# Layer 0's gate pieces moved from the transposes into the scores, a reordered token sum in block 2, and 42 products that nobody reads ahead of waits of TensorE

## The reference, cut to what matters

```python
mod = c_act @ w_ada[l] + b_ada[l]
shift, scale, gate = jnp.split(mod, 3, axis=-1)
h = rmsnorm(x, g_pre[l]) * (1.0 + scale[:, None, :]) + shift[:, None, :]
p = h @ w_in[l]
...
s_raw = jnp.einsum("bthd,bsd->bths", qi_b, k_idx_f)
score = jnp.einsum("bth,bths->bts", w_b, jax.nn.relu(s_raw))
_, sel = lax.top_k(score, k_top)
...
x = x + gate[:, None, :] * rmsnorm(y, g_post[l])
```

## Time and profile before

| | |
|---|---|
| time of 3 runs | 3044.73 us median (3043.07 to 3046.05) |
| the profiled execution's own time | 3046.43 us |
| its span | 3044.6 us |
| granted TensorE clock, mean | 0.98 |
| TensorE busy | 2860.1 us, 94% of the span |
| VectorE busy | 1953.3 us, 64% |
| ScalarE busy | 1323.3 us, 43% |
| GpSimd busy | 1280.0 us, 42% |

### The profile page before, as it was taken

The page is one execution under the profiler, slowest core; times in us unless marked ns, Lnnn a source line. Parts: engine busy times, 40 slices in busy tenths (PEclk is TensorE's granted clock), DMA queues, the critical chain, the costliest instruction groups (busy, mean ns, idle before and its releaser), DMA issues.

```text
span 3044.6 us, 49166 instructions
## 1 busy us (share of the span) xinstructions
PE 2860.1 (94%) x19746; PEld 1749.1 (57%) x19746; DVE 1953.3 (64%) x3140; ACT 1323.3 (43%) x2341; POOL 1280.0 (42%) x1060
## 2 busy tenths in 40 slices
PE   7889998999979988999999999999999999999998
PEld 3438776874429667864466565664764444444443
DVE  3785997763589996644875665666663654444445
ACT  3353654652366646643344554454543322122222
POOL 1302482010602580012545846767661635555551
PEclk9999999999989999999999999999999999999999
DMA  8223241002201340021101111201122201111111
GB/s 292 110 70 122 84 154 52 12 22 104 94 14 43 125 139 29 12 87 59 67 29 42 70 42 42 70 31 66 43 85 110 70 28 56 56 56 44 54 44 74
DMA packets 50898, 213.45 MB, mean 70 GB/s; under 512 B 4680, under 2 KB 9968, under 8 KB 34032
## 3 DMA queue, kind: packets, MB, share of 16 engines
q1 hardware_dynamic: 42288, 195.63, 18.5%
q10 hardware_dynamic: 8384, 14.68, 1.4%
HBM read 190.36 MB, written 19.94 MB: 69 GB/s over the span
## 4 chain that ended last, share of the span: by engine, by line
PE 41%; DVE 3%; POOL 3%; ACT 2%; issue 1%; DMA 0%; ACTq 0%; POOLq 0%; DVEq 0%
PE big L284 7%; PE big L286 7%; PE big L285 7%; PE banks L284 4%; PE banks L286 4%; PE banks L285 4%; PE banks L1183 3%; POOL w_lo L596 2%; PE banks L1162 0%; PE banks L1153 0%; PE banks L1134 0%; PE banks L1164 0%; PE banks L1170 0%; DVE arena L2567 0%; DVE arena L2568 0%
## 5 line engine op out<-in xcount | busy, mean ns | idle before, releaser
L653 POOL TENSOR_TENSOR w_lo<-stage,w_hi 128x512 bf16<-128x512 f32 x340 | 429.7, 1295 | 367.3 <-ACT w_hi L1390 367.0
L646 POOL CAST w_hi<-stage 128x512 bf16<-128x512 f32 x252 | 179.6, 753 | 781.4 <-PE big L286 588.5
L284 PE MATMUL big<-w_hi,ht_hi 128*128 128x256 bf16 (+2 forms) x1280 | 358.0, 288 | 22.7 <-DVE arena L1913 4.7
L596 POOL TENSOR_TENSOR w_lo<-stage,w_hi 128x512 bf16<-128x512 f32 x174 | 249.6, 1445 | 263.6 <-ACT w_hi L1590 263.6
L285 PE MATMUL big<-w_lo,ht_hi 128*128 128x256 bf16 (+2 forms) x1280 | 357.9, 288 | 0.0
L286 PE MATMUL big<-w_hi,ht_lo 128*128 128x256 bf16 (+2 forms) x1280 | 357.8, 287 | 0.0
L284 PE MATMUL big<-ht_hi,w_hi 128*128 128x512 bf16 x816 | 310.2, 380 | 24.7 <-POOL w_lo L596 8.7
L286 PE MATMUL big<-ht_hi,w_lo 128*128 128x512 bf16 x816 | 310.0, 380 | 0.0
L285 PE MATMUL big<-ht_lo,w_hi 128*128 128x512 bf16 x816 | 309.8, 380 | 0.0
L284 PE MATMUL big<-arena,w_hi 128*128 128x512 bf16 (+1 forms) x716 | 222.5, 328 | 21.4 <-DVE arena L2154 8.4
L285 PE MATMUL big<-arena,w_hi 128*128 128x512 bf16 (+1 forms) x716 | 222.6, 328 | 0.0
(11 more groups left out here) (395 smaller groups left out, 7144.2 us busy)
## 6 DMA issues: line engine op xcount, KB each, us to landing
stage<-in_w SPq DMA_DIRECT2D x130, 1024.0 KB, 4.8
arena<-in_w_ada SPq DMA_DIRECT2D x48, 512.0 KB, 4.4
arena<-in_x SPq DMA_DIRECT2D x16, 512.0 KB, 9.2
xs<-arena SPq DMA_DIRECT2D x16, 512.0 KB, 2.6
arena<-xs SPq DMA_DIRECT2D x16, 512.0 KB, 7.2
gt<-arena ACTq DMA_DIRECT2D x16, 256.0 KB, 2.5
arena<-gt ACTq DMA_DIRECT2D x16, 256.0 KB, 2.6
out_x<-arena SPq DMA_DIRECT2D x8, 512.0 KB, 2.6
```

The source lines that it names most:

```text
L284: pe.matmul(out, ah, bh, start=start, stop=False, skip_group_check=onto)
L596: return pool.tensor_tensor(lo, x, hi, ALU.subtract)
L646: pool.tensor_copy(w_flat[0][:, w0 + c0:w0 + c1], stage[:, n % RAW_RING, c0:c1]).then_inc(s_w_hi_split, mark(s_w_hi_split, n, q))
L653: ins = pool.tensor_tensor(w_flat[1][:, w0 + c0:w0 + c1], stage[:, n % RAW_RING, c0:c1], w_flat[0][:, w0 + c0:w0 + c1], ALU.subtract)
```

## The change

Three edits come together.

1. `transpose_x` issues no pieces any more. The 16 gate pieces all run in the scores stage: 3, 3, 4, 3, 3 after blocks 2 to 6. They use `ADA2` and `cb[1]`, a ring of four semaphores of their own, and their first four transfers are issued when the transposes are done. `gate_sum(0)` and `gate_sum(1)` run on VectorE inside block 7 of the scores.
2. In block 2, round 0, VectorE makes the low halves of `t1` between `conv_2(0, 0)` and `conv_2(0, 1)`, and `xs_low(0)` moves behind the first sum of `seven("v", 0)`.
3. `bridge(g, n)` issues n float32 matmuls of 128x512 into a tile that TensorE has just taken; nobody reads them, since the next product starts the tile afresh. There are 5 ahead of `qi`, 6 and 2 ahead of the pairs of `pw2`, 4 ahead of the first logits, and 4 ahead of the last `turn_y`: 21 in each layer.

```diff
         def ada_buf(i):
-            return (ADA if i < 24 else ADA2)[:, i % 4, :, :]
+            return (ADA if i < 16 else ADA2)[:, i % 4, :, :]
+
+        def ada_in(i):
+            return s_ada_in[i % 4 + (4 if i >= 16 else 0)]
...
-            for i in range(16, 24):
-                ada(i)
             sp.wait_ge(s_rb_out, when(s_rb_out))
             sp.dma_start(TOEP, bass.AP(AP_["rb"].tensor, 0, [[1, P], [384, NH], [1, 2 * P]])).then_inc(s_toep_in, mark(s_toep_in, by=16))
             sp.wait_ge(s_gemm, when(s_gemm, "hx", 0, 1, 3))
-            for i in range(24, 28):
+            for i in range(16, 20):
                 ada(i)
...
+            def bridge(g, n):
+
+                for i in range(n):
+                    pe.matmul(g[:, 0:512], ident, con[:, 0:512], start=True, stop=True)
+
...
                     if m == 16:
+                        pe.wait_ge(s_dve_setup, when(s_dve_setup, "cb", 1))
                         ada_at["tile"] = take(pe, "c2", "gate", 0)
...
                         ins.then_inc(s_gemm, mark(s_gemm, "hx", l, half, kp))
-                        ada_pieces(l, 1)
...
-                pe.wait_ge(s_latent_dve, when(s_latent_dve, "cq_lo", l, 1))
                 for n in range(4):
                     g = take(pe, "big", "qi", l, n)
+                    if n == 0:
+                        bridge(g, 5)
+                        pe.wait_ge(s_latent_dve, when(s_latent_dve, "cq_lo", l, 1))
...
                     if tb < NT - 1:
-                        ada_pieces(l, 2 if tb < 5 else 1)
+                        ada_pieces(l, 4 if tb == 4 else 3)
...
                 for n0 in (0, 2):
                     pair = [take(pe, "big", "pw2", l, n) for n in (n0, n0 + 1)]
+                    bridge(pair[0], 6 if n0 == 0 else 2)
...
                 def logits(tb, h):
                     N = (tb + 1) * P
+                    g = take(pe, "big", "lg", l, tb, h)
+                    if tb == 0 and h == 0:
+                        bridge(g, 4)
                     pe.wait_ge(s_qt_lo, when(s_qt_lo, l, tb))
-                    g = take(pe, "big", "lg", l, tb, h)
...
                 def turn_y(tb):
 
+                    g = take(pe, "big", "yt", l, tb)
+                    if tb == NT - 1:
+                        bridge(g, 4)
                     pe.wait_ge(s_ya, when(s_ya, l, tb))
-                    g = take(pe, "big", "yt", l, tb)
...
                 if l == 0:
-                    gate_sum(0)
                     dve.wait_ge(s_ht_lo, when(s_ht_lo, "all", 0))
...
                     w = s_(S_W + tb * 8 + h)
+                    if l == 0 and tb == NT - 1 and h in (2, 4):
+                        gate_sum(h // 2 - 1)
                     dve.wait_ge(s_relu, when(s_relu, l, i))
...
-                if l == 0:
-                    gate_sum(1)
                 count(lambda j: 0.0)
...
                     conv_2(0, 0)
-                    conv_2(0, 1)
                     dve.wait_ge(s_gemm, when(s_gemm, "q", 0, 1))
                     for g in range(2):
                         sum_low(g, "t1", TSB[g])
+                    conv_2(0, 1)
...
-                xs_low(0)
+                if b:
+                    xs_low(0)
...
-                seven("v", b, hgrn, c11=(lambda: xs_low(1),))
+                seven("v", b, hgrn, c11=(lambda: xs_low(1),) if b else (lambda: xs_low(0), lambda: xs_low(1)))
```

More of the change, by code:

```diff
@@ L108, in build @@
         s_act_setup = ctx.enter_context(nc.semaphore("act_setup"))
-        s_ada_in = [ctx.enter_context(nc.semaphore(f"ada_in{i}")) for i in range(4)]
+        s_ada_in = [ctx.enter_context(nc.semaphore(f"ada_in{i}")) for i in range(8)]
         s_ada_used = ctx.enter_context(nc.semaphore("ada_used"))
@@ L491, in ada @@
                 l, n, kp = ADA_PIECES[i]
-                if i >= 4:
+                if i >= 4 and not 16 <= i < 20:
                     sp.wait_ge(s_ada_used, when(s_ada_used, i - 4))
                 sp.dma_start(ada_buf(i), AP_["w_ada"][l, kp * 2 * P:(kp + 1) * 2 * P, n * 512:(n + 1) * 512].rearrange("(k p) n -> p k n", k=2)) \
-                    .then_inc(s_ada_in[i % 4], mark(s_ada_in[i % 4], i, by=16))
+                    .then_inc(ada_in(i), mark(ada_in(i), i, by=16))
             def weights(n):
@@ L539, in _ @@
                 if n == CHUNK_AT[(0, "cv1")]:
-                    for i in range(28, 48):
+                    for i in range(20, 48):
                         ada(i)
@@ L678, in ada_piece @@
                 l, n, kp = ADA_PIECES[i]
-                pe.wait_ge(s_ada_in[i % 4], when(s_ada_in[i % 4], i))
+                pe.wait_ge(ada_in(i), when(ada_in(i), i))
                 for k in (2 * kp, 2 * kp + 1):
-                    ins = pe.matmul(g, cb[l][:, k, :], ada_buf(i)[:, k % 2, :], start=k == 0, stop=k == KT - 1)
+                    ins = pe.matmul(g, cb[i >= 16][:, k, :], ada_buf(i)[:, k % 2, :], start=k == 0, stop=k == KT - 1)
                 ins.then_inc(s_ada_used, mark(s_ada_used, i))
@@ L693, in ada_pieces @@
                     if m == 16:
+                        pe.wait_ge(s_dve_setup, when(s_dve_setup, "cb", 1))
                         ada_at["tile"] = take(pe, "c2", "gate", 0)
                     if m == 24:
-                        pe.wait_ge(s_dve_setup, when(s_dve_setup, "cb", 1))
                         ada_at["tile"] = take(pe, "c2", "gate", 1)
```

## The result

The changed kernel takes 3052.39 us (median of 9 runs, 3048.99 to 3055.20), against 3046.05 us (9 runs) of the kernel before on the same chip. The ratio is 1.0022, with an interval of 1.0014 to 1.0030: it is slower by some 6.7 us. The forecast was 3043.4 us, range 3035 to 3051, and "same" the likeliest; the result lies outside the range, on the slower side.

A forecast was written before the change was run, and what follows sets the result against it. TensorE, busy 94% of the span, was taken as the bound; minus 10.3 (opening) plus 13.8 (scores) minus 3.9 (scores' end) plus 3.1 (bridges) minus 4.0 (block 2) made minus 1.3, so 3043.4 us, range 3035 to 3051.

The forecast's parts named there:

- same: Whole kernel: a time within 0.2%, about 6 us, of the kernel before; chance 0.60.
- The opening: Layer 0's transposes without pieces: VectorE's conversion sets the pace, ending at 63.7 instead of 76.02 us; minus 10.3 net.
- The term for the clock: First projection after the opening: starts at 1.2 GHz because TensorE idles half the time; 2.0 us lost.
- The scores: Scores stage: eight more pieces at 1.72 us each, none hidden since VectorE already idles at each burst; plus 13.8 us.
- the second rival's first leg: Scores: each burst's third piece is half covered, minus 4; part of a rival near 3035 us, chance 0.24.
- The end of the scores: Ahead of conv_in: the gate_sum(1) wait goes, both sums cost 2.5 in block 7, clock gains; minus 3.9 us.
- The clock's part: Behind the last score: the 1.2 GHz stretch from 211.00 to 217.83 runs at 2.4 GHz; minus 2.2 us.
- The third rival: Layer 0 after the scores: the stall passes to VectorE's later search, 3.9 lost and 1 added; 3048 us, chance 0.10.
- The bridges: qi, pw2, first logits and last turn_y: unread products raise the clock but add their length; plus 3.1 us, both layers.
- the first rival's mechanism: At the bridges: they don't buy the clock, low stretches come from small products and stay; 3052 us, chance 0.14.
- Block 2: Block 2, first round: t1 ahead of the second convolution removes TensorE's 4.45 wait; minus 4.0 us, between minus 1 and 7.
- slowed instead: Block 2: VectorE's second convolution, taking the subtractions' place while GpSimd was idle, would be slowed; no size given.

The follow-up runs named there:

- e4_split_later: On the changed kernel, GpSimd's split of the second weight chunk put behind the end of layer 0's opening; 3047.91 us, ratio to before 1.0008.
- e1_pieces: Gate pieces, ring and both gate sums moved as in the changed kernel, no bridges, block 2 as before; 3050.75 us, ratio to before 1.0017.
- e5_open_clock: On e4_split_later, one unread 512-column product ahead of the transposes of the opening's second to eighth tile; ratio to before 1.0012.
- e9_late_halves: On e8_halves, the eight matmuls of the four early pieces placed later in the opening, plus the block 2 edit; 3035.54 us, ratio to before 0.9970.
- e6_gate_sum: On the kernel before, only the second gate sum moved from behind the last score into the last block of scores; 3042.06 us, ratio 0.9989.
- e2_bridges: On the kernel before, all the bridges alone; 3052.18 us, ratio 1.0018.
- e3_sum: On the kernel before, the block 2 edit alone (t1 ahead of the second convolution, xs_low(0) later); 3043.63 us, ratio 0.9989.
- e7_three_bridges: On the kernel before, the bridges of qi, first logits and last turn_y, none at pw2; 3046.93 us, ratio 1.0003.
- e8_halves: e1_pieces with the later second split of e4_split_later, but four pieces kept in the opening, one matmul per tile; 3045.24 us, ratio to before 0.9996.

## Why the prediction was wrong

**The opening: the failed step.** It said "1.97 per tile, 2.05 with waits between the engines", and built 63.7 us from it. The durations came from rows in which GpSimd had nothing to do. The change moves VectorE's work into the 10 us in which GpSimd splits weights, and there both get slower: five pairs of subtractions took 12.77 us (2.81, 2.48, 1.94, 3.06 and 2.48) where five times 1.28 make 6.40. So the overlap cost 6.4 us, and the tiles took 2.6 to 3.7 us each up to 62.79. `e4_split_later` takes one of the two splits away and 3.65 us with it. The sentence that the weights "are split behind other work and are no limit that I can see" looked only at when they are ready and not at what the splitting does to its neighbour.

The forecast missed by less than 6.4 only because its sum had an error the other way. It puts seven pairs of subtractions between the first and the eighth conversion. Each pair stands behind the next tile's conversion, as the two conversions at 46.01 show, so there are six: 1.2 us too much. And a tile that GpSimd leaves alone takes 1.92 us, not 2.05: 0.9 too much. VectorE was through at 67.9 us; less the 6.4 of overlap, an undisturbed opening would end near 61.5, as an estimate. That `e4_split_later` has its record at 63.68, the forecast's own number, is luck: 2.7 us of overlap are left in it, and it began 1.0 us earlier. The term for the clock (2.0) was right in size: 2.4 in the changed kernel and 2.1 in `e4_split_later`.

The Trainium skill has a rule that bears on it and that the forecast did not weigh (SBUF — State Buffer, Who interferes with whom): a VectorE instruction with two inputs in SBUF contends with a GpSimd instruction that reads SBUF, the later one is blocked until the other is done, and one with at most one SBUF input, outside the modes that use both ports, does not contend. The trace agrees: 1.65 and 1.6 us for the subtractions side by side, and an unchanged 0.80 for the conversion.

By the Trainium skill (TensorE: Matmul & The Clock Gate, Part 4), which doesn't count transposes as TensorE being busy, the low level would have lasted through all eight steps. The trace half agrees: it is low from 52.71 to 73.19, over the last three steps, but from 47.00 to 52.70 it is high. In `e1_pieces` it is low from 49.51, back at 2.4 GHz from 52.92 to 56.34 and low again behind that, with nothing but transposes on TensorE since 44.5; there the trace doesn't agree. In `e5_open_clock`, where products stand between the transposes, the projection starts low as well, behind a wait of 4.10 us; in `e9_late_halves`, where products fill most of that wait, it starts high.

**The scores: right.** Plus 13.8 for eight pieces: VectorE's idle time grew by 13.9 us. The cover was used up, and the second rival's first leg is wrong.

**The end of the scores: right in sum, wrong in one part.** The wait gave 3.0 in `e6_gate_sum`, as worked out (4.2 less 1.2). The clock's part (minus 2.2) came from elsewhere: in the changed kernel a low stretch of 3.42 us full of products is still there, behind waits of 1.41 and 1.50 us. The shift fell by 2.1 nevertheless, because a second stretch, 309.99 to 313.40 of before, isn't in the changed kernel. The forecast did not know of that one. The third rival, that the stall passes to VectorE's search, is wrong: the gain stays.

**The bridges: right in mechanism and nearly in size.** The clock is at 2.4 GHz at `pw2`, the logits and `turn_y` (`e2_bridges`), so the first rival's mechanism is wrong, and that the time came out at its 3052 is luck. From the trace they cost 4.2 us behind `conv_in` where the forecast had 4.0. By place, layer 0 and layer 1: `pw2` +3.1 and +3.7 (forecast 2.7 and 3.6), first logits -1.2 and 0 (forecast 0), last `turn_y` -0.7 and -0.4 (forecast -0.7). At `qi`, for which the forecast had -0.9 per layer, the shift hardly moves. Measured alone, all bridges came to 5.5 rather than 3.1, within the interval.

**Block 2: right, 1 us too large.** Forecast minus 4.0, read minus 2.95, measured alone minus 3.3. VectorE sets the time here: TensorE comes 1.6 us earlier by the missing stretch at 1514.89, and waits 6.87 us instead of the 6.03 of `e3_sum`. The stretch behind the wait at 1.2 GHz is 10.24 us instead of 13.65, as expected. The last three steps of VectorE's second convolution took 6.36 us, against 4.70 in the kernel before, with GpSimd's weight sums beside them; those 1.7 us are the "slowed instead" of the forecast, which gave them no number.

**Not foreseen: the entry of block 2.** Plus 3.3 us in one profile and 2.2 in the other. The wait in front is the same in both kernels. Below are TensorE's timelines of before, of the changed kernel, and of its second execution:

```profile
1441.45 0.38 PE L284 MATMUL big<-ht_hi,w_hi 128*128 128x512 bf16 x1 [3.25 <-DVE arena L2366]
```
```profile
1450.02 0.59 PE L284 MATMUL big<-ht_hi,w_hi 128*128 128x512 bf16 x1 [3.28 <-DVE arena L2377]
```
```profile
1450.13 0.38 PE L284 MATMUL big<-ht_hi,w_hi 128*128 128x512 bf16 x1 [3.25 <-DVE arena L2377]
```

Before, the level stays at 2.4 GHz behind 3.25 us; after, it falls behind 3.28 and 3.25. The wait is 3.25 to 3.28 us in every kernel here. The level falls there in `e5_open_clock`, `e6_gate_sum` and `e7_three_bridges` too, and stays up in the other seven. `e6_gate_sum` has no bridge, no moved piece and block 2 as before, so the stretch doesn't need any of these. The second stretch, at 1479, is in both profiles of the changed kernel and in `e5_open_clock` alone. What decides it stays open. No experiment here isolates it.

Sum of the miss: 4.8 opening with its low level, 3.3 entry of block 2, 1.05 block 2, and 1 in the rest make the 10.1 us between minus 1.3 and plus 8.8. By the medians the change is 6.3 us rather than 8.8, as the profiled execution was 2.8 above its median and that of before 0.4.

## What to carry to other kernels

When an edit closes a hole in one engine's row, look at who worked in that hole: VectorE's and GpSimd's durations, read where they took turns, don't hold once they run together. Check a pace against the order of the rows, too: one pair of instructions too many hid a third of the error here. A filler for idle TensorE time is best work that has to be done anyway, cut to the gap and placed where its operand has already arrived (`e9_late_halves` against `e8_halves`); products that nobody reads bought back the clock and, taken together, still cost more than they gave. Measure the parts of a mixed change alone: here two small moves are worth 7 us, and the rest of the change hid them.

## What the runs showed of the hardware

- VectorE's pair of 128x512 subtractions takes 1.28 us with GpSimd idle and 1.94 to 3.06 beside it; GpSimd's four subtractions take 4.5 us alone and 5.86 beside VectorE, its four casts 2.29 and 3.66. Both lose. Single ones of 1.65 and 1.6 us, about the sum of one of each (0.64 and 1.12), look like turns.
- The clock's level behind a wait is not settled by the wait: of 13 profiles with 3.25 to 3.28 us at the entry of block 2, five have 1.2 GHz behind it and eight 2.4. It also fell behind two waits of 1.41 and 1.50 us at the end of the scores.
- Two profiles of the same changed kernel differ in their low stretches: 1.1 us at the entry of block 2, and 1.7 for one near 1117 that only the second has. A part worth 1 or 2 us can't be read from one profile alone.
